# The moving columns of every 256-column fp32r product, read and written in pairs of 16-column lines

## The chip, the cores and the metric

The kernel runs on one core of one Trainium2 chip. The metric is the device time of one execution in microseconds (us). Before the change three executions took 1942.34, 1942.40 and 1946.62 us, the median 1942.4 us. The profiled execution took 1953.66 us.

## The reference

Two stacks of two layers each work on a sequence of 256 positions with 1024 features, in float32. Cut to the large products:

```python
def first_block(x, ...):
    for l in range(DEPTH):                       # DEPTH = 2
        x = x + 0.5 * swiglu_ffn(rmsnorm(x, ffn1_norm[l]), ffn1_w_up[l], ffn1_w_down[l])
        x = x + mixer(rmsnorm(x, mix_norm[l]), w_in[l], b_in[l], ...)
        x = x + 0.5 * swiglu_ffn(rmsnorm(x, ffn2_norm[l]), ffn2_w_up[l], ffn2_w_down[l])
        x = rmsnorm(x, final_norm[l])

def swiglu_ffn(h, w_up, w_down):                 # w_up 1024 x 5632, w_down 2816 x 1024
    a, b = jnp.split(h @ w_up, 2, axis=-1)
    return (jax.nn.silu(a) * b) @ w_down

def second_block(x, ...):
    for l in range(DEPTH):
        p = rmsnorm_2(x, norm1[l]) @ w_in[l]     # q, k, v and a Fourier part
        ...
        x = x + mix @ w_o[l]
        up = dwconv_centred(rmsnorm_2(x, norm2[l]) @ w_up[l], conv_w[l], conv_b[l])
        gate, val = up[..., :D_FF_2], up[..., D_FF_2:]
        x = x + (jax.nn.silu(gate) * val) @ w_down[l]
```

The mixer of the first block has an input projection to queries, keys, values, a gated convolution branch and gates; dilated window attention in three groups; a 31-tap depthwise convolution with a layer norm; and three output projections.

## The kernel before, in words

Activations are kept feature-major: a tensor such as `h_hi` has 128 partitions, then `KT = 8` tiles of 128 features, then `S = 256` positions. A product with a weight matrix has a 128x128 tile of the weights as the stationary operand and the 256 positions as the moving columns. Its result is half of a PSUM bank (a bank has 512 float32 per partition); two such products with neighbouring weight tiles fill one bank.

All weights pass through three rotating slots. A chunk is 16 tiles of 128x128, that is 2048 float32 per partition. SP's queue loads it to `raw`, ScalarE rounds it into `hi` (line 1078, type fp32r), VectorE subtracts and keeps the rest in `lo` (line 1659). The activations are split in the same way (`n_hi` and `n_lo`, `h_hi` and `h_lo`, `hid_hi` and `hid_lo`, `s_hi` and `s_lo`, and others). The helper `mm3` (lines 445 to 449) then issues three products that add up in PSUM: high weights with high activations (line 447), high weights with low activations (448), low weights with high activations (449). Each of them has its own weight load, so that a weight load and a product alternate in TensorE's program.

`pairs` is the most frequent caller: one chunk, eight k-tiles by two output halves by three products, 48 in all. `down`, `last_down`, `project`, `project2`, `chunk_quarters`, `fourier_project` and `sequence_dft` are others with 256 moving columns. `value_chunk` and `dft_part` call `mm3` with the roles exchanged: the activation is stationary, and 512 columns of the weight chunk move. The value projection of the second block moves 128 columns. The feed-forward parts (`ffn`) run 33 chunks each: up-chunks into banks 0 and 1, and a down-chunk for every second of them, which accumulates in banks 2 to 5. The first feed-forward part of a layer (`ffn(0, ...)`) and the second (`ffn(FFN2_0, ...)`) of the first block have the same loop, the same slots, buffers and banks.

The order on TensorE is written out by hand, and each chunk waits for its `lo` semaphore. Other products (statistics, scores, transposes, attention values) are plain float32 and don't go through `mm3`.

Of the kernel before, what the change touches and what calls it, by code (L numbers as in the profile page):

```python
# [28 lines left out]
S = 256  # L29
# [9 lines left out]
HALF = TAPS // 2  # L39
EPS = 1e-6  # L40
NEG = -1e30


TAPS_GLU, TAPS_QK, TAPS_V = 10, 6, 4
# [190 lines left out]
def build(nc, d):  # L235
# [204 lines left out]
    def pe_program(pe):  # L440
        cnt = Count(dict(lo=SLOTS))
        first = {}
        mm = nc.tensor.matmul

        def mm3(out, w_hi, w_lo, a_hi, a_lo, start=False):

            mm(out, w_hi, a_hi, start=start, stop=False, skip_group_check=True)  # L447
            mm(out, w_hi, a_lo, start=False, stop=False, skip_group_check=True)  # L448
            return mm(out, w_lo, a_hi, start=False, stop=True, skip_group_check=True)  # L449
# [7 lines left out]
        def gates_and_values(t):  # L457

            c, out = GATE0 + t, bank[GATE_BANKS[t % 2]]
            take("lo")  # L460
            late = late_spread_at(t)
            for k in range(KT):
                if k == KT // 2 and c in ADDED:
                    take(f"added{c % SLOTS}", 16)
                if k == 2 and t:
                    value_pair(t - 1)
                if late and (k == 7 or (k == 4 and t)):
                    if t == 0:
                        take("v")
                    late_spread(late.pop(0))  # L470
                for j in range(2):
                    last = mm3(out[:, j * S:(j + 1) * S], tile(hi, c, 2 * k + j), tile(lo, c, 2 * k + j),
                               h_hi[:, k, :], h_lo[:, k, :], start=(k == 0 and j == 0))
            last.then_inc(sem["pe"], 1)

        def pairs(c, out, k0, nk, a_hi, a_lo, start, ready=None, stat_after=None, by_halves=False, added=False,
                  final_after=None):

            if by_halves:
                pe.wait_ge(sem["lo0a"], 1)  # L480
            else:
                take("lo")
            for k in range(nk):
                if by_halves and k == KT // 2:
                    take("lo")
                if added and k == KT // 2:
                    take(f"added{c % SLOTS}", 16)
                if k == stat_after:
                    summed_stat()
                if k == final_after:  # L490
                    final_stat(bank[6][:, 0:S], 1)
                if ready and k % 2 == 0:
                    take(ready)
                for j in range(2):
                    last = mm3(out[:, j * S:(j + 1) * S], tile(hi, c, 2 * k + j), tile(lo, c, 2 * k + j),
                               a_hi[:, k0 + k, :], a_lo[:, k0 + k, :], start=start and k == 0 and j == 0)
            last.then_inc(sem["pe"], 1)
# [15 lines left out]
        def down_tile(c, k, m, h_hi, h_lo, start=False):  # L513
            return mm3(bank[2 + m // 2][:, (m % 2) * S:(m % 2 + 1) * S], tile(hi, c, 8 * k + m),
                       tile(lo, c, 8 * k + m), h_hi[:, k, :], h_lo[:, k, :], start=start)
# [1897 lines left out]
    with nc.Block() as block:  # L2413
        @block.sync
        def _(sp):
            sp_program(sp)
            sp.wait_ge(sem["x"], 4 + L * (PER_LAYER1["x"] + PER_LAYER2["x"]))
            sp.dma_start(d["out"], sq[:, :, :]).then_inc(sem["out"], 16)
            sp.wait_ge(sem["out"], 16)

        @block.tensor
        def _(pe):
            pe_program(pe)

        @block.scalar
        def _(act):
            act_program(act)

        @block.vector
        def _(v):  # L2430
            dve_program(v)

        @block.gpsimd
        def _(pool):
            pool_program(pool)
# [42 lines left out]
def _constants():  # L2478
# [17 lines left out]
    for qt in range(2):  # L2496
# [5 lines left out]
        at = C["mask1"] + qt * 2 * S  # L2502
        c[:, at:at + 2 * S] = np.where(np.concatenate(valid, axis=1), 0, NEG)
        q = (qt * P + i)[:, None]
        at = C["mask2"] + qt * S
        c[:, at:at + S] = np.where(np.abs(q - np.arange(S)[None, :]) <= 128, 0, NEG)
    c[:, C["eps"]], c[:, C["eps2"]] = EPS, EPS * EPS
# [98 lines left out]
```

## Time and profile before

| | |
|---|---|
| median of three runs | 1942.4 us (1942.34 to 1946.62) |
| the profiled execution | 1953.66 us, of it 1951.7 us the span of the trace |
| TensorE products busy | 1906.9 us, 98% of the span, 15852 of them |
| TensorE weight loads busy | 1837.7 us, 94%, 15852 of them |
| VectorE busy | 1467.1 us, 75% |
| ScalarE busy | 1105.0 us, 57% |
| GpSimd busy | 41.7 us, 2% |
| granted TensorE clock, mean | 0.997 |
| HBM read | 359.68 MB, 185 GB/s over the span |

A busy share says how much of the span an engine had some instruction in flight. The products of TensorE are pipelined: one record is longer than the distance from its start to the next one's, so the distance of the starts, and not the record's duration, tells what a product costs in a dense stretch. "PE" is TensorE's products, "PEld" its weight loads, "DVE" VectorE, "ACT" ScalarE.

### The profile page before, as it was taken

To read this page: it belongs to the slowest core of one execution; us is meant where nothing else is said; L and a number is where in the kernel's file an instruction comes from. 1 tells how busy PE (TensorE), PEld (TensorE's weight loads), DVE (VectorE), ACT (ScalarE), POOL (GpSimd) and SP (SyncE) were. 2 spreads that over 40 slices of the span, in tenths; PEclk is the share of its full clock that TensorE was granted. 3 is DMA by queue.
4 is the path that set the end of the run, shared out by engine and by line. 5 is a ranking of instruction groups with operands and counts; after the bars stand their busy time and mean duration, and the time that the engine had idled before them with its cause. 6 is when DMAs were issued, how large, how long until landed. Compare 5 with 4: busy or idle time off the path is not lost.

```text
span 1951.7 us, 38913 instructions
## 1 busy us (share of the span) xinstructions
PE 1906.9 (98%) x15852; PEld 1837.7 (94%) x15852; DVE 1467.1 (75%) x2147; ACT 1105.0 (57%) x1414; POOL 41.7 (2%) x52
## 2 busy tenths in 40 slices
PE   7999999999999999999999999999999999999998
PEld 7999898899999999998997999999889999889998
DVE  5555799987765585568999877656888778878777
ACT  5444666676544464446676765444656556556554
POOL 0000011000000000000110000000000000000000
PEclk9999999999999999999999999999999999999999
DMA  6556599634665545556996346555335554335554
GB/s 256 200 178 222 191 295 285 172 105 145 209 215 192 192 173 191 177 209 215 281 263 184 90 150 231 199 193 180 125 118 188 191 193 166 130 123 190 192 192 152
DMA packets 62732, 368.59 MB, mean 189 GB/s; under 512 B 8096, under 2 KB 8352, under 8 KB 25888
## 3 DMA queue, kind: packets, MB, share of 16 engines
q1 hardware_dynamic: 54704, 339.37, 50.0%
q0 software_dynamic: 6912, 25.17, 7.2%
q10 hardware_dynamic: 1008, 2.51, 0.3%
q8 instruction: 80, 1.31, 0.3%
q14 instruction: 28, 0.23, 0.0%
HBM read 359.68 MB, written 1.05 MB: 185 GB/s over the span
## 4 chain that ended last, share of the span: by engine, by line
PE 74%; DVE 17%; ACT 4%; DMA 3%; issue 2%; SPq 0%; DVEq 0%; ACTq 0%
PE bank L447 23%; PE bank L448 22%; PE bank L449 22%; DVE lo L1659 5%; DVE cv L1912 5%; ACT hi L1078 2%; DVE zt L1875 1%; DMA zt<-zt 1%; PE bank L629 1%; DMA lo<-in_w 1%; PE bank L656 1%; ACT n_hi L1140 1%; PE bank L642 1%; PE bank L614 1%; DVE qk L1877 1%
## 5 line engine op out<-in xcount | busy, mean ns | idle before, releaser
L1659 DVE TENSOR_TENSOR lo<-raw,hi 128x2048 fp32r<-128x2048 f32 (+1 forms) x336 | 663.9, 1977 | 197.6 <-ACT hi L1078 196.9
L1078 ACT ACTIVATE hi<-raw 128x2048 fp32r<-128x2048 f32 (+1 forms) x336 | 598.7, 1784 | 103.5 <-PE bank L449 89.6
L447 PE MATMUL bank<-n_hi,hi 128*128 128x256 f32 x2256 | 635.7, 282 | 21.0 <-DVE lo L1939 12.2
L448 PE MATMUL bank<-n_lo,hi 128*128 128x256 f32 x2256 | 629.0, 279 | 0.0
L449 PE MATMUL bank<-n_hi,lo 128*128 128x256 f32 x2256 | 628.9, 279 | 0.0
L447 PEld LDWEIGHTS bank<-n_hi,hi 128*128 128x128 f32 x2256 | 427.5, 189 | 27.0 <-DVE lo L1939 12.2
L448 PEld LDWEIGHTS bank<-n_lo,hi 128*128 128x128 f32 x2256 | 424.6, 188 | 1.3 <-issue 1.0
L449 PEld LDWEIGHTS bank<-n_hi,lo 128*128 128x128 f32 x2256 | 425.8, 189 | 0.0
L447 PE MATMUL bank<-h_hi,hi 128*128 128x256 f32 x1152 | 330.8, 287 | 6.3 <-DVE h_lo L1663 4.0
L448 PE MATMUL bank<-h_lo,hi 128*128 128x256 f32 x1152 | 321.4, 279 | 0.0
L449 PE MATMUL bank<-h_hi,lo 128*128 128x256 f32 x1152 | 321.3, 279 | 0.0
L447 PE MATMUL bank<-hid_hi,hi 128*128 128x256 f32 x928 | 258.7, 279 | 0.5 <-DVE lo L1659 0.5
L448 PE MATMUL bank<-hid_lo,hi 128*128 128x256 f32 x928 | 258.5, 279 | 0.0
L449 PE MATMUL bank<-hid_hi,lo 128*128 128x256 f32 x928 | 258.5, 279 | 0.0
L447 PEld LDWEIGHTS bank<-h_hi,hi 128*128 128x128 f32 x1152 | 218.3, 189 | 20.1 <-issue 14.6
L448 PEld LDWEIGHTS bank<-h_lo,hi 128*128 128x128 f32 x1152 | 218.3, 190 | 0.5
L449 PEld LDWEIGHTS bank<-h_hi,lo 128*128 128x128 f32 x1152 | 218.4, 190 | 0.0
L1166 ACT ACTIVATE silu_t<-up_t 128x256 f32<-128x256 f32 x88 | 36.8, 418 | 295.1 <-DVE up_t L1736 295.1
L1912 DVE SCALAR_TENSOR_TENSOR cv<-upad,prm,cv 128x256 f32<-128x256 f32 x480 | 195.4, 479 | 0.0
L447 PEld LDWEIGHTS bank<-hid_hi,hi 128*128 128x128 f32 x928 | 175.5, 189 | 0.9 <-DVE lo L1659 0.9
L449 PEld LDWEIGHTS bank<-hid_hi,lo 128*128 128x128 f32 x928 | 174.8, 188 | 0.0
L448 PEld LDWEIGHTS bank<-hid_lo,hi 128*128 128x128 f32 x928 | 174.2, 188 | 0.0
(271 smaller groups left out, 2325.7 us busy)
## 6 DMA issues: line engine op xcount, KB each, us to landing
raw<-in_w SPq DMA_DIRECT2D x286, 1024.0 KB, 4.9
raw<-in_w SPq DMA_DIRECT2D x53, 512.0 KB, 3.8
lo<-in_w POOLq DMA_DIRECT2D x48, 512.0 KB, 8.8
zt<-zt SPq DMA_DIRECT2D x96, 64.0 KB, 6.7
bv<-in_bv SPq DMA_DIRECT2D x2, 768.0 KB, 6.2
spread<-in_spread SPq DMA_DIRECT2D x2, 768.0 KB, 8.0
x<-in_x ACTq DMA_DIRECT2D x4, 256.0 KB, 10.1
out_x<-sq SPq DMA_DIRECT2D x1, 1024.0 KB, 3.9
```

Source lines behind the costliest of these rows:

```text
L447: mm(out, w_hi, a_hi, start=start, stop=False, skip_group_check=True)
L448: mm(out, w_hi, a_lo, start=False, stop=False, skip_group_check=True)
L449: return mm(out, w_lo, a_hi, start=False, stop=True, skip_group_check=True)
L614: last = mm(bank[LN_BANK][:, j * S:(j + 1) * S], spread[:, at:at + P], rstd[:, 1, :], start=True, stop=True)
L629: last = mm(bank[3 + e][:, at:at + n], qk[r, 4 * g + hp, qt * P:(qt + 1) * P], qk[r, 12 + 4 * g + hp, cols], start=(g == 0), stop=True, sk ...
L642: last = nc.tensor.transpose(bank[5 + e][:, b * P:(b + 1) * P], p_sb[:, e, b * P:(b + 1) * P], ident)
L656: last = mm(bank[Y_BANK][e * HD:(e + 1) * HD, qt * P:(qt + 1) * P], v_sb[:, kt, v:v + HD], pt_sb[:, e, b, :], start=(b == 0), stop=(b == 3 ...
L1078: fn(hi[:, s, 0:w], raw[:, s, 0:w], ACT.Copy).then_inc(sem["hi"], 1)
L1140: last = fn(out, part, ACT.Copy, scale=gain(t))
L1166: fn(silu_t[:, u, :], gate_of[:, u, 0, :], ACT.Silu).then_inc(sem["silu"], 1)
L1659: v.tensor_tensor(lo[:, s, 0:w], raw[:, s, 0:w], hi[:, s, 0:w].bitcast(F32), ALU.subtract)\
L1912: ins = v.scalar_tensor_tensor(cv[:, t, :], src, w, cv[:, t, :], ALU.mult, ALU.add)
```

## The change

`mm3` passes its result and both moving operands through a new helper. Where the last dimension has 256 elements, these are seen as two halves (`h`) of 8 lines (`j`) of 16 elements (`i`), and walked in the order line, half, element: elements 0 to 15, 128 to 143, 16 to 31, 144 to 159, and so on. 128 float32 are 512 bytes and 16 are 64 bytes. The result is written in the same order, so every value stands where it stood before. Products with 512 or 128 moving columns, stationary operands, and all products outside `mm3` are as before. The number of instructions, their order and their waits are the same.

```diff
+LINE = 16
...
+        def by_lines(t):
+
+            if t.shape[-1] != S:
+                return t
+            return t.rearrange("p (h j i) -> p j h i", h=2, i=LINE)
+
         def mm3(out, w_hi, w_lo, a_hi, a_lo, start=False):
 
+            out, a_hi, a_lo = by_lines(out), by_lines(a_hi), by_lines(a_lo)
             mm(out, w_hi, a_hi, start=start, stop=False, skip_group_check=True)
             mm(out, w_hi, a_lo, start=False, stop=False, skip_group_check=True)
             return mm(out, w_lo, a_hi, start=False, stop=True, skip_group_check=True)
```

## Rows read from the trace of the kernel before

**Rows 1.** The page: busy us, share of the span, instructions; then shares of the chain.

```profile
PE 1906.9 (98%) x15852; PEld 1837.7 (94%) x15852; DVE 1467.1 (75%) x2147; ACT 1105.0 (57%) x1414; POOL 41.7 (2%) x52
...
PE bank L447 23%; PE bank L448 22%; PE bank L449 22%; DVE lo L1659 5%; DVE cv L1912 5%; ACT hi L1078 2%; DVE zt L1875 1%; DMA zt<-zt 1%; PE bank L629 1%; DMA lo<-in_w 1%; PE bank L656 1%; ACT n_hi L1140 1%; PE bank L642 1%; PE bank L614 1%; DVE qk L1877 1%
```

**Rows 2.** Groups of instructions by form, TensorE: shapes xcount | busy us, mean ns.

```profile
L447 PE MATMUL bank<-n_hi,hi 128*128 128x256 f32 x2256 | 635.7, 282 | 21.0 <-DVE lo L1939 12.2 <-DVE lo L1659 6.7 <-DVE n_lo L1713 1.5
...
L447 PE MATMUL bank<-h_hi,hi 128*128 128x256 f32 x1152 | 330.8, 287 | 6.3 <-DVE h_lo L1663 4.0 <-DMA lo<-in_w 2.2
...
L447 PE MATMUL bank<-hid_hi,hi 128*128 128x256 f32 x928 | 258.7, 279 | 0.5 <-DVE lo L1659 0.5
...
L447 PE MATMUL bank<-s_hi,hi 128*128 128x256 f32 x128 | 35.3, 276 | 0.0
...
L447 PE MATMUL bank<-yt_hi,hi 128*128 128x256 f32 x64 | 18.1, 282 | 0.0
...
L447 PE MATMUL bank<-hi,g_hi 128*128 128x256 f32 x32 | 9.7, 302 | 0.0
```

**Rows 3.** Busy time by stretch, all engines: window, us, busy us (xcount) by engine.

```profile
40.00:160.00 120.00, 120.00 (x1021) 120.00 (x1020) 71.42 (x66) 53.26 (x52) 0.00 (x0) 1.00 0.55 193
540.00:660.00 120.00, 120.00 (x1061) 120.00 (x1060) 72.42 (x67) 54.04 (x53) 0.00 (x0) 1.00 0.57 195
281.00:431.00 150.00, 146.36 (x1190) 130.65 (x1190) 139.93 (x274) 101.77 (x149) 12.95 (x15) 0.99 0.74 201
...
950.00:1110.00 160.00, 155.64 (x1267) 139.98 (x1266) 147.88 (x293) 109.00 (x157) 13.79 (x16) 0.99 0.75 202
```

**Rows 4.** Timeline of products, second feed-forward part of layer 0: start us, duration us.

```profile
599.86 0.28 PE L447 MATMUL bank<-n_hi,hi 128*128 128x256 f32 x1
...
600.88 0.28 PE L447 MATMUL bank<-n_hi,hi 128*128 128x256 f32 x1
```

**Rows 5.** Timeline of products, first feed-forward part of layer 0.

```profile
59.80 0.28 PE L448 MATMUL bank<-n_lo,hi 128*128 128x256 f32 x1
...
60.98 0.28 PE L449 MATMUL bank<-n_hi,lo 128*128 128x256 f32 x1
```

**Rows 6.** Busy time by stretch, products alone: three stretches, then three others.

```profile
20.00:190.00 170.00, 169.48 (x1436) 1.00 0.57 202
690.00:870.00 180.00, 178.87 (x1511) 1.00 0.54 191
1478.00:1658.00 180.00, 179.95 (x1522) 1.00 0.54 184
510.00:670.00 160.00, 159.98 (x1407) 1.00 0.58 201
1191.00:1351.00 160.00, 160.00 (x1411) 1.00 0.57 197
1790.00:1940.00 150.00, 150.00 (x1326) 1.00 0.55 192
```

**Rows 7.** Timeline of weight loads in the stretch of rows 4.

```profile
599.87 0.19 PEld L448 LDWEIGHTS bank<-n_lo,hi 128*128 128x128 f32 x1
599.98 0.19 PEld L449 LDWEIGHTS bank<-n_hi,lo 128*128 128x128 f32 x1
```

**Rows 8.** Timeline of products with 128 moving columns through the same helper.

```profile
1389.81 0.28 PE L447 MATMUL bank<-hi,n_hi 128*128 128x128 f32 x1
...
1390.92 0.28 PE L448 MATMUL bank<-lo,n_hi 128*128 128x128 f32 x1
```

**Rows 9.** Timeline of products with 512 moving columns, two stretches.

```profile
223.62 0.39 PE L447 MATMUL bank<-hi,n_hi 128*128 128x512 f32 x1
...
225.00 0.39 PE L447 MATMUL bank<-hi,n_hi 128*128 128x512 f32 x1
...
203.14 0.40 PE L447 MATMUL bank<-hi,n_hi 128*128 128x512 f32 x1
...
203.84 0.40 PE L447 MATMUL bank<-hi,n_hi 128*128 128x512 f32 x1
```

**Rows 10.** The chain in order of time: start us, us, sixteen plain float32 product records.

```profile
434.35 3.65 PE bank L727 x16
```

## The prediction

> **What bounds the kernel now.** I read the page first: TensorE's products are busy 98% of the span, and the three lines of `mm3` alone hold 23 + 22 + 22 = 67% of the chain that ended last; the reader is to see that no other line has more than 5% [rows 1]. Then the groups by form, for how many products the change touches. Line 447 has 2256, 1152, 928 and 128 products in its four large groups with 256 moving columns [rows 2]; five smaller groups (96, 64, and three of 32) bring it to 4720 [rows 2], and lines 448 and 449 have as many each: 14,160 of 15,852. Then busy time by stretch, for who is bound where: in the feed-forward parts TensorE is busy for every one of 120 us and VectorE for 71 to 72, while around the attention of the first block VectorE has 139.93 of 150 us and 147.88 of 160 us, so that it shares the bound there [rows 3]. Last the timelines, because only the distance of two starts is a price.
>
> That distance has two values. In the second feed-forward part of layer 0, nine products lie between 599.86 and 600.88 us: 113.3 ns each [rows 4]. In the first feed-forward part, ten lie between 59.80 and 60.98 us: 118 ns [rows 5]. The counts by stretch say that each value holds for a whole stretch: 1436, 1511 and 1522 products in 170, 180 and 180 us against 1407, 1411 and 1326 in 160, 160 and 150 us, which is 118 against 113 [rows 6]. The granted clock is 1.00 in all six, the 2.4 GHz level, at which 256 columns are 106.7 ns. So a product costs 6.6 ns more than its columns at the short pace and 11 ns more at the long one: if I read it as per line of 16 columns, 0.42 ns, one column's time. That is what the change can act on, at most 14,160 x 6.6 = 93 us of the short pace's excess, and about 20 us of the long one's: the three long-paced stretches are 530 us, 530 / 0.118 = 4,490 products, times 4.5 ns.
>
> **The change, part by part.** It removes no instruction and adds none, nor a wait or a DMA; ScalarE, VectorE and the queues do the same work in the same order. Three things change inside a product.
>
> First, the order in which lines of the moving operand are read. Is the excess made by one line following its neighbour, which the jump of 512 bytes would alter? The trace speaks against it twice. The two feed-forward parts of layer 0 have the same code, slots, buffers and banks, so the same addresses, and differ by 4.5 ns in each product [rows 4, 5]: what separates them is not the addresses but how the stream started. And the 512-column products take (225.00 - 223.62) / 6 = 230 ns in one place and (203.84 - 203.14) / 3 = 233 ns in another, although both read contiguous columns [rows 9]; again two paces for one kind of read. At 512 columns the excess over 213.3 ns is 17 to 20 ns, so it grows with the columns and is not the weight load, which hides there. This looks like a rate at which four-byte columns are supplied, with a phase. Such a rate asks how many lines are read, and that number stays 16. I take nothing for this edit. The bounds: on the gain side the product can't go below what its weight load lets it. Each load starts 10 ns after a product's start, by rounded figures, and the next product follows a full period later [rows 4, 7]; and the 128-column products, whose own columns are only 53 ns at this clock, still start (1390.92 - 1389.81) / 10 = 111 ns apart [rows 8]. So at best 113.3 becomes 111. On the loss side no row has a broken walk. The next slower product in the trace is the plain float32 record with 256 columns: sixteen in 3.65 us, at most 228 ns [rows 10]. Between 111 and 228 I choose the present value, being within 3 ns of the near end, and by the argument above.
>
> The Trainium skill ("Advanced Engine Details and Errata", SBUF Cachelines) says that full speed needs at least two hits on a 16-byte line, and that only leaving a line on each access is penalised. A run of 16 float32 is four full lines, so by that page this read costs what it did; no row here has a shorter run to try it on.
>
> Second, the order in which the result is written. A plain float32 record writes as many columns as an fp32r product, and accumulates too, at half the pace [rows 10], so no row tells whether PSUM has room for a jump. I take nothing, with the same far end of 228 ns; the loss would have to come from the 16 jumps, and if each costs one column's time it is 16 x 0.42 = 6.7 ns.
>
> Third, the pattern has three free dimensions in place of one. If the walk costs a column's time at each wrap, that is the same 6.7 ns, and if it is worked out ahead of the stream, nothing. TensorE has an instruction in flight in every one of the 120 us of a feed-forward stretch [rows 3], so the next one is known long before its turn, and I take nothing.
>
> The sum is 0 us on the profiled execution's 1953.66 us (its span of 1951.7 and 2 us around it). That execution lies 11 us above the median. One whole stretch that changes from one pace to the other is worth some 1,500 x 4.5 = 7 us, so paces that flip between executions could explain it; I carry the change of 0 to the median: **1942.4 us**. The paces are what makes even this uncertain: were every stretch at the short one the time would be 20 us less, were every one at the long one (14,160 - 4,490) x 4.5 = 43 us more. As they follow from how the stream starts, and its starts are unchanged, I let this case run from 1936 to 1950.
>
> **The rivals.**
>
> *A price per jump (slower).* Each of the 16 line changes in a product costs one column's time more, on the read side, in PSUM or in the walk itself. For it speaks that the present excess is so near to one column per 16; against it that a stream of columns might be fetched by whole lines, whose number stays. The price is 14,160 x 6.7 = 94 us. In the attention stretches, where VectorE is at 92 to 93% [rows 3], some 1,900 products can be partly absorbed; I take off half of theirs, 6 us. That gives 1942.4 + 88 = 2030 us. It decides from about 0.4 ns a product, which is 6 us, the bound of what a measurement of this kernel can tell from no change (0.3%). Its tail is long: at 228 ns a product the time would be above 3500 us, which I hold for very unlikely.
>
> The Trainium skill ("Advanced Engine Details and Errata", PSUM Cachelines) says "Any non-contiguous AP significantly slows down matmuls", and that two consecutive elements should be contiguous for best throughput. The first sentence would make this rival the outcome; the second is fulfilled by runs of 16. No row of this trace shows a broken PSUM walk, so the chance of this rival is not small.
>
> *The line conflict is real (faster).* Neighbouring lines do get in each other's way, lines 512 bytes apart do not, and the product falls to the pace of its weight load, 111 ns, in all stretches: 14,160 x 2.3 = 33 us and the long pace's 20 us more, 53 us in all, 1889 us. For it speaks that the excess is so close to one column's time in 16 and needs no weight load [rows 9]; against it the two paces at equal addresses. Should this happen, next late would be VectorE in the attention stretches, which would take back a few us. [...]
>
> *A lottery of paces.* The products keep their prices but the broken walk shifts how a stretch locks in: from 20 us less to 43 us more, as above. For it speaks that the paces are decided at each start; against it that three runs lie within 4.3 us of each other. I share it out to both sides of the first case and to the two rivals' chances.
>
> **How the numbers follow.** No change of price 0.42, price per jump 0.33, faster 0.25, each with its part of the lottery. Of the first, 0.03 goes to either side of 0.3%: faster 0.28, same 0.36, slower 0.36. The likeliest case alone is 1936 to 1950 us. The range that should hold 8 times in 10 reaches to both rivals: 1885 us, just beyond the pace of the weight load, to 2035 us, just beyond one column's time per jump.
>
> **What would show it.** In the trace after, starts 113.3 ns apart in the stretch of rows 4 show the first case; 120 ns the price per jump; 111 ns or less the conflict. The 512-column products are untouched and must stay at 229 to 233 ns; if they move, it is the paces and not the walk. VectorE's and ScalarE's durations must stay. I am wrong if the 256-column products change by over half a nanosecond while stretches keep their pace, and wrong on the mechanism if the long pace of the first feed-forward part goes.

## The result: 3% slower, one pace in place of two

The changed kernel takes 2004.97 us (2001.55 to 2006.37, four runs) against 1943.22 us (1942.34 to 1946.62, four runs): a ratio of 1.0297, with a 95% interval from 1.0252 to 1.0342. The forecast was 1942.4 us, its likeliest case 1936 to 1950 us; its rival on the slower side had said 2030 us. The time lies inside the wide range (1885 to 2035 us) only because that range was stretched to the rivals, which is no merit of the mechanism that was forecast.

The page of the changed kernel: busy time, then the chain that ended last.

```profile
PE 1966.3 (98%) x15852; PEld 1899.3 (95%) x15852; DVE 1469.6 (73%) x2147; ACT 1106.2 (55%) x1414; POOL 41.8 (2%) x52
...
PE bank L455 28%; PE bank L457 27%; PE bank L456 27%; DVE lo L1667 2%; DMA lo<-in_w 1%; ACT hi L1086 1%; PE bank L664 1%; PE bank L637 1%; PE bank L650 1%; ACT n_hi L1148 1%; PE bank L600 1%; PE bank L622 1%; PE bank L848 0%; PE bank L877 0%; PE bank L611 0%
```

Against [rows 1] the number of instructions is the same and VectorE, ScalarE and GpSimd are busy as long as before (1469.6 against 1467.1 us, 1106.2 against 1105.0); only TensorE grew, by 59 us. The three lines of `mm3` now hold 82% of the chain instead of 67%, and VectorE's lines, of which the page before showed 5%, 5%, 1% and 1%, are down to 2%: around the attention the chain now runs mostly through TensorE.

The timeline of products of the changed kernel (start us, duration us), in the second feed-forward part of layer 0 and in the first one:

```profile
600.13 0.28 PE L455 MATMUL bank<-n_hi,hi 128*128 128x256 f32 x1
600.25 0.28 PE L456 MATMUL bank<-n_lo,hi 128*128 128x256 f32 x1
...
600.73 0.28 PE L457 MATMUL bank<-n_hi,lo 128*128 128x256 f32 x1
```

```profile
59.81 0.28 PE L455 MATMUL bank<-n_hi,hi 128*128 128x256 f32 x1
...
60.77 0.28 PE L457 MATMUL bank<-n_hi,lo 128*128 128x256 f32 x1
```

Both are 120.0 ns apart: (600.73 - 600.13) / 5 and (60.77 - 59.81) / 8. The 113.3 ns of [rows 4] became 120.0, and so did the 118 ns of [rows 5]. Busy time by stretch of the changed kernel (window, us, busy us with the count, clock, DMA share, GB/s) says the same of whole stretches:

```profile
40.00:160.00 120.00, 120.00 (x1002) 120.00 (x1001) 70.51 (x65) 51.58 (x51) 0.00 (x0) 1.00 0.55 191
...
288.00:440.00 152.00, 149.27 (x1191) 133.91 (x1190) 137.62 (x269) 102.50 (x151) 12.07 (x14) 1.00 0.73 197
972.00:1132.00 160.00, 158.66 (x1268) 142.83 (x1267) 148.21 (x293) 109.33 (x157) 13.81 (x16) 1.00 0.74 201
```

The count in a window is the handiest gauge of pace, and the rest of this document uses it. Some two products are already under way when a window opens, so the pace is 120 us / (count - 2): 1061 is 113.3 ns, 1021 is 117.8, 1002 is 120.0, 1012 is 118.8. A feed-forward stretch of 120 us held 1021 or 1061 products before [rows 3]. Now it holds 1002 in four of the six feed-forward parts and a few less in the last two, where TensorE pauses for a moment; between the pauses the starts are 120.0 ns apart there too. These are the last two:

```profile
1520.00:1640.00 120.00, 119.89 (x999) 1.00 0.54 184
1810.00:1930.00 120.00, 119.89 (x996) 1.00 0.53 184
```

Around the attention of layer 1 the same work, 1267 products and 293 VectorE instructions, takes 160 us before [rows 3] and 160 us after. TensorE had 4.4 us of waiting there (155.64 us busy) and now has 1.3 (158.66): the longer products went into time in which it had waited for VectorE, and nothing was lost. Around the attention of layer 0 nearly the same work (1190 products, now 1191) took 150 us and takes 152.

That accounts for the 48 us between the two profiled spans (1951.7 and 1999.7 us). The three feed-forward parts that ran at the short pace lose 3 x 1,584 x 6.7 ns = 32 us, the three at the long pace 3 x 1,584 x 2.2 ns = 10 us, and the remaining 6 us are left for the 4,660 products elsewhere. The medians are 62 us apart and not 48: the profiled execution of the kernel before lay 10 us above its median, that of the changed kernel 3 us below.

### The profile page after: what moved, and what is told of

It reads as the page before. It is cut to its first block, busy times and chain, and to the rows that moved or that the text cites. A ratio compares the mean times of both kernels' runs of the same rounds, so it can differ in the third digit from the quotient of the medians.

```text
span 1999.7 us, 38913 instructions
## 1 busy us (share of the span) xinstructions
PE 1966.3 (98%) x15852; PEld 1899.3 (95%) x15852; DVE 1469.6 (73%) x2147; ACT 1106.2 (55%) x1414; POOL 41.8 (2%) x52
## 4 chain that ended last, share of the span: by engine, by line
PE 89%; DVE 6%; ACT 3%; DMA 2%; issue 1%; DVEq 0%; ACTq 0%; SPq 0%
PE bank L455 28%; PE bank L457 27%; PE bank L456 27%; DVE lo L1667 2%; DMA lo<-in_w 1%; ACT hi L1086 1%; PE bank L664 1%; PE bank L637 1%; PE bank L650 1%; ACT n_hi L1148 1%; PE bank L600 1%; PE bank L622 1%; PE bank L848 0%; PE bank L877 0%; PE bank L611 0%
## 5 line engine op out<-in xcount | busy, mean ns | idle before, releaser
L1086 ACT ACTIVATE hi<-raw 128x2048 fp32r<-128x2048 f32 (+1 forms) x336 | 598.5, 1783 | 130.6 <-PE bank L457 122.4
L455 PE MATMUL bank<-n_hi,hi 128*128 128x256 f32 x2256 | 645.9, 286 | 16.1 <-DVE lo L1947 11.4
L457 PE MATMUL bank<-n_hi,lo 128*128 128x256 f32 x2256 | 640.1, 284 | 0.0
L456 PE MATMUL bank<-n_lo,hi 128*128 128x256 f32 x2256 | 640.1, 284 | 0.0
L456 PEld LDWEIGHTS bank<-n_lo,hi 128*128 128x128 f32 x2256 | 430.9, 191 | 1.3 <-issue 1.0
L457 PEld LDWEIGHTS bank<-n_hi,lo 128*128 128x128 f32 x2256 | 430.7, 191 | 0.0
L457 PE MATMUL bank<-h_hi,lo 128*128 128x256 f32 x1152 | 326.2, 283 | 0.0
L456 PE MATMUL bank<-h_lo,hi 128*128 128x256 f32 x1152 | 325.6, 283 | 0.0
L455 PE MATMUL bank<-hid_hi,hi 128*128 128x256 f32 x928 | 263.1, 284 | 0.2
L456 PE MATMUL bank<-hid_lo,hi 128*128 128x256 f32 x928 | 262.9, 283 | 0.0
L457 PE MATMUL bank<-hid_hi,lo 128*128 128x256 f32 x928 | 262.9, 283 | 0.0
```

The lines of the kernel that those rows point to most:

```text
L1086: fn(hi[:, s, 0:w], raw[:, s, 0:w], ACT.Copy).then_inc(sem["hi"], 1)
```

## The experiments

All but two are edits of the changed kernel; `e7_repeat_line` and `e9_repeat_2d` are edits of the kernel before. "Ratio" is the time against that of the kernel before in runs beside the experiment, with a 95% interval in brackets. Where no ratio is given, the run has a single time, and the argument rests on its paces. Of each run the windows 40 to 160 us and 540 to 660 us are shown, products alone; both lie in feed-forward parts of layer 0. The kernel before has 1021 and 1061 there.

**Read side or write side.**

```diff
-            out, a_hi, a_lo = by_lines(out), by_lines(a_hi), by_lines(a_lo)
+            a_hi, a_lo = by_lines(a_hi), by_lines(a_lo)      # e1_read_only
+            out = by_lines(out)                              # e2_write_only
```

> The moving operands of every 256-column product are read in lines as in the changed kernel, the result is written straight through, so the columns of each result stand permuted (this kernel's values are not the reference's). Theory R (the 16 line jumps on the read side cost the changed kernel its 120.0 ns a product): 120.0 ns here too, 2005 us. Theory W (the jumps of the result in PSUM cost it): 113.3 and 117.8 ns as before, 1943 us. Theory D (the walk over three dimensions costs it, whichever operand has it): 120.0 ns, 2005 us, as R; the flat walk of three dimensions tells these two apart.

> The result of every 256-column product is written in lines, the moving operands are read straight through, so the columns of each result stand permuted (this kernel's values are not the reference's). Theory R (read jumps): 113.3 and 117.8 ns, 1943 us. Theory W (PSUM jumps): 120.0 ns, 2005 us. Theory D (three dimensions on either operand): 120.0 ns, 2005 us.

Reads alone in lines, then the result alone in lines:

```profile
40.00:160.00 120.00, 120.00 (x1003) 1.00 0.54 191
540.00:660.00 120.00, 120.00 (x1002) 1.00 0.53 190
```

```profile
40.00:160.00 120.00, 120.00 (x1061) 1.00 0.57 205
540.00:660.00 120.00, 120.00 (x1062) 1.00 0.55 196
```

Read side: 2004.25 us (2003.82 to 2006.12), ratio 1.0292 [1.0275, 1.0309], the whole loss. Write side: 1942.53 us, ratio 0.999 [0.9965, 1.0016], nothing. The second pair shows one thing more. Its first window runs at the short pace, where the kernel before had the long one; no operand of its reads differs. So the pace of a stretch isn't given by its reads; a kernel executed twice, further down, shows that it isn't in the code at all.

**Dimensions or breaks.**

```diff
-            return t.rearrange("p (h j i) -> p j h i", h=2, i=LINE)
+            return t.rearrange("p (j h i) -> p j h i", h=2, i=LINE)
```

> Operands and result have the same three free dimensions of 8, 2 and 16, but in the order in which they lie in memory, so that nothing jumps. Theory D (each wrap of the walk costs): 120.0 ns a product, 2005 us. Theories R and W (the jump itself costs): 113.3 and 117.8 ns, 1943 us. If the program's patterns are merged into one run before they reach the engine, the trace shows 256 columns in one dimension and this run tells nothing.

```profile
40.00:160.00 120.00, 120.00 (x1021) 1.00 0.54 194
540.00:660.00 120.00, 120.00 (x1062) 1.00 0.55 195
```

1947.39 us (1939.78 to 1959.24), ratio 1.0004 [0.9976, 1.0032]. The instruction records carry a pattern of 256 elements in one dimension: the walk had been merged, so, as foreseen, this run tells nothing of dimensions. It is a second copy of the kernel before, and as such useful below. The test of dimensions came with the next pair. It changes the kernel before, on the read side alone, and reads the same columns over and over (the values are then not the reference's):

```diff
+            return t[:, 0:S // 2].rearrange("p (j i) -> p j i", i=LINE).unsqueeze(2).broadcast_to([P, S // 2 // LINE, 2, LINE])   # e7
+            return t[:, 0:LINE].unsqueeze(1).broadcast_to([P, S // LINE, LINE])                                                  # e9
```

> The first 8 lines of 16 columns of each moving operand are each read twice in a row, the other 8 are not read, the result is written straight through (this kernel's values are not the reference's). The walk has the same counts, 16, 2 and 8, but goes back by 64 bytes or on by none instead of 448 back and 512 on. Theory R-far (the distance of the jump, the other place in memory, costs): 113.3 or 117.8 ns, 1943 us. Theory D (any walk of more than one dimension costs on the moving side): 120.0 ns, 2005 us.

> The moving operand of every 256-column product is its first 16 columns, sixteen times over, in a walk of two dimensions (16 by 16, the outer step zero); the result is written straight through (this kernel's values are not the reference's). Theory N (the number of short runs sets the price, whatever the number of dimensions and the distance): 120.0 ns a product and 2003 us, as with three dimensions. Theory D3 (the third dimension costs): 113.3 or 117.8 ns, 1945 us. Theory F (each new 64-byte line that is fetched costs, so that a line already fetched costs less): below 113 ns.

Each line twice (three dimensions), then the first line sixteen times (two dimensions):

```profile
40.00:160.00 120.00, 120.00 (x1002) 1.00 0.53 191
540.00:660.00 120.00, 120.00 (x1002) 1.00 0.53 189
```

```profile
40.00:160.00 120.00, 120.00 (x1003) 1.00 0.53 191
540.00:660.00 120.00, 120.00 (x1003) 1.00 0.54 191
```

2002.72 and 2000.52 us. The distance of the jump has no part in it, nor which memory is read (sixteen columns, over and over, cost as much), nor the number of dimensions. What is common to all the kernels at 120.0 ns so far is that the moving walk consists of 16 runs of 16.

**How long a run, how many of them.** `LINE` was set to 64, 32, 8 and 4, all else as in the changed kernel.

```diff
-LINE = 16
+LINE = 32   # e4_line32; 64 in e5_line64 and e16_line64_timed, 8 in e6_line8, 4 in e14_line4
```

> As the changed kernel, with lines of 32 columns (128 bytes): 8 runs instead of 16, still 512 bytes apart. Theory J (each run costs one column's time, 0.42 ns, above the 113.3 ns): 113.3 + 8 x 0.42 = 116.7 ns, about 1943 + (14,160 x 116.7 - (8,000 x 113.3 + 6,160 x 117.8)) / 1000 = 1943 + 20 = 1963 us if the long pace is gone as in the changed kernel. Theory P (any broken walk falls into one fixed pace of 120.0 ns): 120.0 ns, 2005 us.

> As the changed kernel with lines of 64 columns: 4 runs a product, 512 bytes apart. So far 1 run gave 113.3 (or 117.8), 8 runs 118.8, 16 runs 120.0 ns. Theory S (a step at the first break, then a slope of (120.0 - 118.8) / 8 = 0.15 ns a run): 118.2 ns, 1981 us. Theory J (a price per jump that levels off, nothing at no jump): between 115 and 117 ns, 1950 to 1970 us.

> As the changed kernel with lines of 8 columns (32 bytes): 32 runs. Theory S (step and slope): 120.0 + 16 x 0.15 = 122.4 ns, 2037 us. Theory L (what costs is leaving a 64-byte line, of which 16-column runs leave as many as any order): 8-column runs leave twice as many, so another 6.7 ns or more, 126.7 ns or above, about 2095 us.

> As the changed kernel with lines of 4 columns: 64 runs. Theory FIX (a fixed price of 6 to 7 ns per product with a little per run, 0.2 ns): 120 + 48 x 0.2 = 130 ns at most, under 2140 us. Theory RUN (a price per 64-byte line opened, so that 4-column runs open a line four times): 120 + 48 x 0.42 = 140 ns or more, above 2280 us.

> The kernel with runs of 64 columns again, timed: if long runs are free, the ratio to the kernel before holds 1.000 in its interval, and the products are 113.3 or 117.8 ns apart.

The windows for runs of 64, 32, 8 and 4 columns, in this order:

```profile
40.00:160.00 120.00, 120.00 (x1021) 1.00 0.54 194
540.00:660.00 120.00, 120.00 (x1062) 1.00 0.55 195
```

```profile
40.00:160.00 120.00, 120.00 (x1012) 1.00 0.54 192
540.00:660.00 120.00, 120.00 (x1013) 1.00 0.54 192
```

```profile
40.00:160.00 120.00, 120.00 (x975) 120.00 (x975) 68.29 (x63) 50.12 (x50) 0.00 (x0) 1.00 0.52 184
540.00:660.00 120.00, 120.00 (x1002) 120.00 (x1001) 70.04 (x68) 54.73 (x52) 0.00 (x0) 1.00 0.54 189
```

```profile
40.00:160.00 120.00, 120.00 (x950) 1.00 0.51 182
540.00:660.00 120.00, 120.00 (x947) 1.00 0.51 181
```

| run length | runs | pace in the two windows, ns | 117.8 + 0.14 x runs | time, us (the kernel before, beside it) |
|---|---|---|---|---|
| 256 (before) | 1 | 117.8 and 113.3 | | 1943.22 |
| 64 | 4 | 117.8 and 113.3 | | 1942.69 (1952.98); timed again 1948.23 (1948.37), ratio 0.9997 [0.9968, 1.0026] |
| 32 | 8 | 118.8 | 118.9 | 1988.89 (1946.94), ratio 1.0211 [1.0194, 1.0228] |
| 16 (the change) | 16 | 120.0 | 120.0 | 2004.97 (1943.22) |
| 8 | 32 | 123.3 and 120.0 | 122.3 | 2039.87 (1952.98) |
| 4 | 64 | 126.7 | 126.8 | 2093.14 (1948.37) |

Runs of 64 columns are free, both paces included. From 32 columns down no window has 113.3 ns any more. The line in the fourth column, the long pace of before plus 0.14 ns a run, is my fit: it meets the walks of 8, 16 and 64 runs, but not that of 32, which has two paces again, 1 ns above the line in one window and 2.3 ns below it in the other, where runs of 8 cost no more than runs of 16. So the price is not a fixed one per jump, while the split of the 6.7 ns that a short-paced product lost, into 4.5 for the lost pace and 2.2 for sixteen runs, is a reading of the fit and not shown.

Of the theories, J (116.7 ns) and P (120.0) both missed the 118.8 of 32-column runs. S and J had put the first step at a broken walk as such, and both were wrong on 64. For 8-column runs S's 122.4 ns and 2037 us came near the mean and the time, though not to either pace, and L's 126.7 is out. Of 4-column runs, theory FIX's bound of 130 ns held and RUN's 140 didn't.

The 64-column kernel was profiled twice, and this is the plainest evidence that the pace isn't in the code. Two of its windows in the first execution (`e5_line64`), then the same two in the second (`e16_line64_timed`):

```profile
740.00:860.00 120.00, 120.00 (x1061) 1.00 0.56 202
1520.00:1640.00 120.00, 120.00 (x1061) 1.00 0.53 188
```

```profile
740.00:860.00 120.00, 120.00 (x1021) 1.00 0.54 193
1520.00:1640.00 120.00, 120.00 (x1021) 1.00 0.51 182
```

Same kernel, other pace: 113.3 ns in both stretches, then 117.8 in both. The two executions were on different chips, so these profiles alone don't exclude the chip as the cause; but ten executions of this kernel on one chip still spread from 1940.81 to 1955.5 us.

**512 columns.** The walk is applied only where 512 columns move, the rest is as before the change.

```diff
-            if t.shape[-1] != S:
+            if t.shape[-1] != 2 * S:
                 return t
-            return t.rearrange("p (h j i) -> p j h i", h=2, i=LINE)
+            return t.rearrange("p (h j i) -> p j h i", h=4, i=LINE)   # LINE 16, 64, 32 in e8, e12, e15
```

> The 256-column products are as before the change; the 384 products with 512 moving columns are read and written in 32 lines of 16 columns, neighbours 512 bytes apart. They ran at 229 to 233 ns. Theory M (the price belongs to the moving stream alone): 32 runs cost twice what 16 do, 229 + 13 = 242 ns, and the time goes up by 384 x 13 = 5 us. Theory C (the price comes from reading while a weight load, some 110 of the 229 ns, reads too): 6 to 7 ns, 236 ns, and 2.5 us.

> Only the 512-column products are broken, into 8 runs of 64 columns. With 256 columns, 4 runs of 64 were free and 8 runs of 32 cost 5.5 ns. Theory LEN (the length of a run decides, 64 is long enough): 229 to 233 ns as before. Theory CNT (the number of breaks decides): about 5 ns more, 235 ns, as with 32 runs of 16.

> Only the 512-column products are broken, into 16 runs of 32 columns. 32 runs of 16 made 229 to 235 ns, 8 runs of 64 made nothing. Theory FIX (a fixed price once runs are shorter than 64 columns): 234 to 235 ns. Theory RUN (in proportion to the number of runs): 232 ns. Theory DOUBLE (5.5 ns per 8 runs of 32, as with 256 columns): 240 ns.

The timelines of the value projection with runs of 16, 64 and 32:

```profile
218.91 0.40 PE L455 MATMUL bank<-hi,n_hi 128*128 128x512 f32 x1
...
221.05 0.40 PE L455 MATMUL bank<-hi,n_hi 128*128 128x512 f32 x1
```

```profile
222.57 0.39 PE L455 MATMUL bank<-hi,n_hi 128*128 128x512 f32 x1
...
223.95 0.39 PE L455 MATMUL bank<-hi,n_hi 128*128 128x512 f32 x1
```

```profile
213.99 0.40 PE L457 MATMUL bank<-hi,n_lo 128*128 128x512 f32 x1
...
216.09 0.40 PE L457 MATMUL bank<-hi,n_lo 128*128 128x512 f32 x1
```

Nine steps of 238 ns, six of 230, nine of 233. Over all their 512-column products the first has 235.3 ns in the mean and the third 233.8, against 229.8 in the kernel before. Eight runs of 64 cost nothing here and eight of 32 cost 5.5 ns there, so at eight runs it is their length that decides, not their number. Runs of 32 take the short pace (229) away and leave the long one (233). Runs of 16 go beyond it: many of their stretches are at 236 to 237 ns. The 235.3 ns is what theory C had said (236), but its reason, a price that arises beside the weight load, isn't borne out by the next pair; of e15's theories FIX (234 to 235) came nearest. The times (1957.81, 1941.86 and 1950.83 us) lie within what the kernel before itself takes from run to run, 1937.96 to 1961.49 us, and say nothing.

**The weight load.** The second and third product of a group use half of their weight columns.

```diff
+            wide_s = out.shape[-1] == S          # e11 keeps the line with by_lines behind this one, e10 has none
+            n = HD if wide_s else P              # HD = 64
-            mm(out, w_hi, a_lo, start=False, stop=False, skip_group_check=True)
-            return mm(out, w_lo, a_hi, start=False, stop=True, skip_group_check=True)
+            mm(out[0:n], w_hi[:, 0:n], a_lo, start=False, stop=False, skip_group_check=True)
+            return mm(out[0:n], w_lo[:, 0:n], a_hi, start=False, stop=True, skip_group_check=True)
```

> Contiguous walks as before the change, but the second and third product of each group of three with 256 columns use only the first 64 columns of their weights and write half of the partitions (the other half of those two terms is left out). So two of three weight loads are half as long, and fall beside the first and the second product. Theory B (the product waits for its neighbour's weight load or shares reads with it): the first two of three fall to 107 to 111 ns, the third stays at 113 or 118. Theory M (the moving stream alone sets the pace): all three stay at 113.3 or 117.8 ns.

> The walk of the changed kernel with the same two halved weight loads (half of the partitions of two of the three terms is left out). Theory B (the price of short runs arises beside the weight load): the first two of three products fall well under 120 ns, by 3 ns or more, the third stays at 120. Theory M (it belongs to the moving stream): all three stay at 120.0 ns, 2005 us.

The timelines, contiguous and in lines; a form 128*64 is a product with half the weights:

```profile
599.75 0.28 PE L455 MATMUL bank<-n_hi,hi 128*128 128x256 f32 x1
599.86 0.28 PE L457 MATMUL bank<-n_lo,hi 128*64 128x256 f32 x1
...
600.65 0.28 PE L458 MATMUL bank<-n_hi,lo 128*64 128x256 f32 x1
```

```profile
599.79 0.28 PE L459 MATMUL bank<-n_hi,lo 128*64 128x256 f32 x1
...
600.75 0.28 PE L458 MATMUL bank<-n_lo,hi 128*64 128x256 f32 x1
```

The loads did become shorter, though not by half (0.19 us, then 0.13; timeline of the contiguous run):

```profile
599.98 0.19 PEld L455 LDWEIGHTS bank<-n_hi,hi 128*128 128x128 f32 x1
600.09 0.13 PEld L457 LDWEIGHTS bank<-n_lo,hi 128*64 128x64 f32 x1
```

Eight steps of 113 ns, eight of 120: the pace is the same in both walks, as theory M had it, and theory B's fall doesn't come. I had set the near bound of the forecast, 111 ns, by the weight load, and these runs show that it was not what held the stream at 113.3.

**One of three.** Only the middle product of a group has the broken walk.

```diff
-            out, a_hi, a_lo = by_lines(out), by_lines(a_hi), by_lines(a_lo)
...
-            mm(out, w_hi, a_lo, start=False, stop=False, skip_group_check=True)
+            mm(by_lines(out), w_hi, by_lines(a_lo), start=False, stop=False, skip_group_check=True)
```

> Only the second of each group of three products (high weights, low activations) has the changed kernel's walk, on its moving operand and its result. Theory OWN (the price belongs to the broken product itself): that product is followed after 120 ns, the other two after 113.3 or 117.8: 1943 + 4,720 x 5 = 1967 us. Theory NEXT (the price arises in the handover to a product whose walk is broken): the distance from the first product to the second is the long one. Theory BOTH: two of three distances grow.

```profile
40.00:160.00 120.00, 120.00 (x1003) 1.00 0.54 191
540.00:660.00 120.00, 120.00 (x1012) 1.00 0.53 187
```

1994.56 us, not 1967. Over the run the distances are 117.6, 119.5 and 121.1 ns after the first, second and third product, 119.4 in the mean, against 115.1 to 115.4 after each of the three in the kernel before. Theory OWN is out: it wanted 120 after the second product alone. NEXT is out too: the distance from the first to the second is the shortest of the three over the run. BOTH can't be told apart so plainly. The first window has 116, 122 and 122 ns, two long ones of three; the second has 119.2, 117.5 and 120, all three above 113.3. Either way a third of the short-run products costs nearly the price of all (119.4 against 120.0 ns): here the pace belongs to the stream and not to the product.

## Why the prediction was wrong, point by point

*What bounds the kernel* was right: the products of `mm3`, with VectorE sharing the bound around the attention, where nothing was lost in layer 1 and about 2 us in layer 0.

*The reading order, priced at nothing: this step failed.* The argument was that the excess over the columns' own time is a rate of supply, which asks how many lines are read, and that number stays 16. The runs show that it isn't the number of lines but the length of the unbroken run: one line read sixteen times costs 120.0 ns, and 4 runs of 64 columns nothing. The term measured +62 us where the sum had 0: the read-only run has the whole loss (ratio 1.0292), the write-only run none. What I had inferred of the two paces was right as far as it went, that addresses don't decide them, and the 64-column kernel executed twice bore it out. From "not the addresses" I concluded "not the walk", which doesn't follow: I should have asked what a harder walk does to the better pace. The prediction had named this as its own sign of a wrong mechanism, that the long pace of the first feed-forward part goes, and it went. Its controls held: the 512-column products kept their mean (229.5 ns, before 229.8), and VectorE and ScalarE their busy times.

By the SBUF Cachelines section of the Trainium skill ("Advanced Engine Details and Errata") a run of four full lines is at full speed. For this operand the measurement decides otherwise: 16 float32 in a run, four full lines, made 120.0 ns, 32 made 118.8, and 64 were the shortest of the lengths tried that kept 113.3.

*The writing order, priced at nothing,* was right: 0.999 [0.9965, 1.0016]. The PSUM Cachelines section of the same page of the Trainium skill says in one sentence that any non-contiguous pattern slows products significantly, which this run contradicts, and in the next that every two consecutive elements should lie together for the best throughput, which it agrees with, for runs of 16.

*The dimensions of the walk, priced at nothing,* were right: on the read side two and three dimensions with the same runs have the same 120.0 ns, and three dimensions with runs of 64 are free.

*The rival "a price per jump"* had the side and, at 120 ns, the pace after, but the wrong mechanism and a time of 2030 us. That its 120 ns came out was luck: the same rule gives 116.7 ns for 8 jumps and 126.7 for 32, and the runs have 118.8, and 120.0 or 123.3. Its mis-sized term is 14,160 x 6.7 ns: it charged the full amount to products at the long pace too, which lost 2.2 ns. With the 4,490 that the prediction itself had counted there, that alone is 4,490 x 4.5 = 20 us of the 25 that it was too high.

*The rival "line conflict"* is refuted: reading one line only, with no neighbour, costs as much.

*The lottery of paces* was in the sum as a width, and its event came about in a way that I had not listed: not all stretches short or all long, but both paces gone, the short one and the long one, with 120.0 ns in place of either.

What stays open is the mechanism beneath: why 64 columns in a run are enough and 32 are not, what makes a stretch with long runs take 113.3 or 117.8 ns, and why runs of 8 have two paces again where runs of 16 have one.

## What to carry to other kernels

Keep the moving operand of fp32r products in runs of at least 64 columns, the shortest that cost nothing here, with 256 and with 512 columns; where a layout forces shorter ones, pay for it on the result's side, which took runs of 16 for nothing. When a dense stream shows two paces at equal code, treat the better one as fragile, and ask of an edit what it does to each pace separately. And read pace from counts in equal windows: a change of 1% in a product's price is plain there, where the time of a run hides it.

## What the runs showed that I had not expected

The kernel before varies from 1937.96 to 1961.49 us over its runs beside the experiments. The lottery of paces fits this, though only profiled executions can show it. In six windows of 120 us, one in each feed-forward part, the profiled execution of the kernel before (span 1951.7 us) has three at the long pace, and the write-only kernel (span 1939.8 us) one:

```profile
740.00:860.00 120.00, 120.00 (x1021) 1.00 0.55 195
1220.00:1340.00 120.00, 120.00 (x1062) 1.00 0.56 194
1520.00:1640.00 120.00, 120.00 (x1021) 1.00 0.53 183
1810.00:1930.00 120.00, 120.00 (x1061) 1.00 0.55 191
```

```profile
740.00:860.00 120.00, 120.00 (x1021) 1.00 0.55 197
1220.00:1340.00 120.00, 120.00 (x1061) 1.00 0.56 196
1520.00:1640.00 120.00, 120.00 (x1061) 1.00 0.53 188
1810.00:1930.00 120.00, 119.65 (x1056) 1.00 0.51 181
```

Two parts of 1,584 products at 4.5 ns are 14 us by this estimate, and the spans differ by 12. The changed kernel has one pace and varies by 5 us (2001.55 to 2006.37). And one product in three with short runs is enough to take the short pace from the other two.
